# Expert weights in a two-layer diffusion trunk: down rows laid four to a partition, gate/up columns regrouped to match

## The reference, cut to what matters

```python
def expert_choice_ffn(h, w_router, w_gate, w_up, w_down):   # 16 experts, D = D_EXPERT = 1024
    xt = h.reshape(n, D)
    cap = EC_FACTOR * n // N_EXPERTS        # 64 sample tokens or 16 prompt tokens for each expert
    gate, idx = lax.top_k(softmax(xt @ w_router).T, cap)
    xe = jnp.take(xt, idx, axis=0)
    hid = jax.nn.silu(einsum('ecd,edf->ecf', xe, w_gate)) * einsum('ecd,edf->ecf', xe, w_up)
    ye = einsum('ecf,efd->ecd', hid, w_down) * gate[..., None]
    y = zeros.at[idx].add(ye)
```

## Time and profile before

| | |
|---|---|
| median of three runs | 3452.91 us |
| lowest, highest | 3452.17, 3455.37 us |
| the profiled execution, first to last instruction | 3453.8 us |
| TensorE busy | 3344.3 us, 97% |
| VectorE, ScalarE, GpSimd busy | 1257.7, 677.4, 183.0 us |
| mean rate of the DMA engines | 194 GB/s over the span |
| the same in an expert stage | 391 to 393 GB/s |

### The profile page before, as it was taken

One profiled execution on the slowest core, in us unless ns is written; L12 is line 12 of the kernel. 1 busy time (PEld: TensorE's weight loads), 2 busy tenths in 40 slices (PEclk: granted clock), 3 DMA queues, 4 the chain that ended last, 5 costly groups with the idle time before them and its releaser, 6 DMA issues.

```text
span 3453.8 us, 47737 instructions
## 1 busy us (share of the span) xinstructions
PE 3344.3 (97%) x20975; PEld 1901.5 (55%) x20975; DVE 1257.7 (36%) x2317; ACT 677.4 (20%) x1410; POOL 183.0 (5%) x283
## 2 busy tenths in 40 slices
PE   6999999999999899999989999999999998999998
PEld 3557767765654544443355577677656555434433
DVE  3455443436442321212143545433363523111213
ACT  3131111114332300000021311111143322000001
POOL 1000000001100000000100000000011000000000
PEclk9999999999999899999999999999999999999999
DMA  7332332332242799999952324233422418999997
GB/s 224 104 113 66 98 95 65 104 96 90 66 151 80 253 386 390 391 392 385 384 152 78 115 65 122 71 79 90 114 71 92 157 49 310 388 397 390 393 386 300
DMA packets 219086, 669.28 MB, mean 194 GB/s; under 512 B 10574, under 2 KB 24086, under 8 KB 215552
## 3 DMA queue, kind: packets, MB, share of 16 engines
q1 hardware_dynamic: 199200, 613.97, 50.3%
q0 software_dynamic: 13248, 36.65, 3.9%
q10 hardware_dynamic: 6432, 15.62, 1.2%
HBM read 603.04 MB, written 63.15 MB: 193 GB/s over the span
## 4 chain that ended last, share of the span: by engine, by line
PE 91%; DMA 5%; ACT 2%; DVE 1%; issue 1%; SPq 0%; ACTq 0%; DVEq 0%
PE unit L902 13%; PE unit L1426 12%; PE unit L850 11%; PE work L1429 9%; PE work L1426 6%; PE unit L914 4%; PE unit L893 3%; PE unit L933 3%; PE unit L1298 3%; DMA ring<-in_w_e_gate 3%; PE unit L844 3%; PE work L1139 2%; PE work L1105 2%; PE unit L860 1%; PE unit L1251 1%; PE unit L1310 1%
## 5 line engine op out<-in xcount | busy, mean ns | idle before, releaser
L902 PE MATMUL unit<-hT,ring 128*128 128x512 f32 x1024 | 480.2, 597 | 0.0
L1426 PE MATMUL unit<-ring,arena 128*64 128x512 f32 x1568 | 355.2, 598 | 5.4 <-DMA ring<-in_w_e_gate 4.1
L1429 PE MATMUL work<-ring,arena 128*32 128x256 f32 x4608 | 274.8, 382 | 0.4 <-DMA ring<-in_w_e_gate 0.4
L2390 DVE SCALAR_TENSOR_TENSOR arena<-work,arena 32x256 f32<-32x256 f32 x128 | 61.6, 482 | 552.9 <-PE work L1429 551.5
L902 PEld LDWEIGHTS unit<-hT,ring 128*128 128x128 f32 x1024 | 179.0, 192 | 140.1 <-issue 140.1
L1426 PEld LDWEIGHTS unit<-ring,arena 128*64 128x64 f32 x1568 | 109.3, 137 | 226.7 <-issue 214.5
L1429 PEld LDWEIGHTS work<-ring,arena 128*32 128x32 f32 x4608 | 136.8, 109 | 159.8 <-issue 80.4
L850 PE MATMUL unit<-hT,ring 128*128 128x512 f32 x512 | 221.1, 592 | 0.0
L1921 ACT ACTIVATE arena<-work 128x512 f32<-128x512 f32 x32 | 19.1, 597 | 850.3 <-PE work L1443 850.3
L1426 PE MATMUL work<-ring,arena 128*64 128x512 f32 x736 | 166.5, 594 | 2.1 <-ACT arena L1922 2.1
L850 PE MATMUL unit<-arena,ring 128*128 128x512 f32 x384 | 166.8, 592 | 0.0
(11 more groups left out here) (448 smaller groups left out, 4637.2 us busy)
## 6 DMA issues: line engine op xcount, KB each, us to landing
ring<-in_w_e_gate SPq DMA_DIRECT2D x50, 2048.0 KB, 14.8
ring<-in_w_e_up SPq DMA_DIRECT2D x48, 2048.0 KB, 13.8
ring<-in_w_e_down SPq DMA_DIRECT2D x46, 2048.0 KB, 15.3
ring<-in_w_in SPq DMA_DIRECT2D x32, 2048.0 KB, 16.1
ring<-in_w_ada SPq DMA_DIRECT2D x24, 2048.0 KB, 8.7
arena<-in_w_e_down SPq DMA_DIRECT2D x18, 2048.0 KB, 14.1
arena<-in_w_e_up SPq DMA_DIRECT2D x16, 2048.0 KB, 13.5
arena<-in_w_e_gate SPq DMA_DIRECT2D x14, 2048.0 KB, 16.2
```

The costliest lines, as they stand in the source:

```text
L902: last = mm(bank[:, :], w[:, k, m * P:(m + 1) * P], hT[:, k, 0:TS], start=k == 0, stop=k == KD - 1)
L1426: last = mm(big[SLS * c:SLS * c + SLS, :], x, w[:, kk, 512 * c:512 * c + 512], start=k == 0, stop=k == KD - 1)
L1429: last = mm(low[SLOTP * c:SLOTP * c + SLOTP, 0:256], xp, w[:, kk, 256 * c:256 * c + 256], start=k == 0, stop=k == KD - 1)
L2390: STT(y[SLS:SLS + SLOTP, 256 * c:256 * c + 256], W[5][r, 0:256], gpro[r, e:e + 1], gatep[r, :], ALU.mult, ALU.mult)
```

## The change

The load of a down chunk takes the same 512 rows, but partition p now gets the rows 4p to 4p + 3 of the half, which are 16 KB in a row in memory. Block kk of the slot is therefore row 512 half + 4p + kk. The loads of gate and up are as before.

The hidden values have to be turned so that partition p of `hidT` holds these rows. For the samples this is done in `turn_hidden`: tile m takes every fourth column of `hid`. For the prompt tokens it is done earlier: the gate and up matmuls of the narrow part stream their 256 weight columns with a step of four words (16 bytes), two such series after one another, so that the output group c holds the columns 512 (c // 2) + 4a + 2 (c % 2) + m at place 128m + a. The output itself is written in order. The down matmuls stream contiguous columns as before. The numbers of instructions, their widths, the semaphores and their order are the same.

```diff
                 for q, (e, part) in enumerate(MOE):
-                    w = A[dict(g="w_e_gate", u="w_e_up", d="w_e_down")[part[0]]][l, e].rearrange("(k p) n -> p k n", p=P)
+                    w = A[dict(g="w_e_gate", u="w_e_up", d="w_e_down")[part[0]]][l, e]
                     half = int(part[1])
-                    load(l * LAYER_CHUNKS + PRE_CHUNKS + q, w[:, 4 * half:4 * half + 4, :], n=D)
+                    rows = w[512 * half:512 * half + 512, :]
+                    load(l * LAYER_CHUNKS + PRE_CHUNKS + q, rows.rearrange("(p k) n -> p k n", p=P) if part[0] == "d"
+                         else rows.rearrange("(k p) n -> p k n", p=P), n=D)
...
-                                else:
+                                elif kind == "d":
                                     last = mm(low[SLOTP * c:SLOTP * c + SLOTP, 0:256], xp,
                                               w[:, kk, 256 * c:256 * c + 256], start=k == 0, stop=k == KD - 1)
+                                else:
+                                    cols = w[:, kk, 512 * (c // 2):512 * (c // 2) + 512].rearrange("p (a m) -> p m a", m=4)
+                                    out = low[SLOTP * c:SLOTP * c + SLOTP, 0:256].rearrange("p (m a) -> p m a", m=2)
+                                    last = mm(out, xp, cols[:, 2 * (c % 2):2 * (c % 2) + 2, :],
+                                              start=k == 0, stop=k == KD - 1)
...
                     for m in range(4):
-                        tr(W[0][:, tile_t(m)], hid[:, tile_t(m)], ident)
+                        tr(W[0][:, tile_t(m)], hid.rearrange("p (a m) -> p m a", m=4)[:, m, :], ident)
```

## The result

The changed kernel takes 3686.07 us, the median of four runs (3682.90 to 3689.52), against 3453.53 us for the kernel before (3452.17 to 3455.37, four runs). The ratio is 1.0676 with a 95% interval of 1.0661 to 1.0691. The prediction was 3678 us with a range of 3446 to 3712.

A forecast was written before the change was run, and what follows sets the result against it. TensorE was taken as the bound, with the DMA engines just able to follow. 3453.8 + 217 (streamed step) + 11.5 (transposes) - 4.5 (waits) = 3677.8, given as 3678 us (+6.5%), range 3446 to 3712.

The forecast's parts named there:

- What bounds the kernel: Expert stages: TensorE leads, busy 100.00 of 100 us; the DMA engines are just able to follow.
- Part 2: Narrow gate and up blocks: streaming weight columns with a step of four words doubles a column's time, +217 us.
- the row: VectorE's reduction at line 2283, stepping 32 words: 1.74 ns a value, read as a memory limit holding for TensorE too.
- Part 3: Sample transposes: a stepped stationary operand adds up to 90 ns to each of 128 weight loads, +11.5 us.
- Part 1: Down loads in 16 KB runs: 4.5 us of TensorE's waits in the expert stages gone, at most 6.1 us.
- Step free: Rival: stepped gate, up and transpose reads cost 0, only the DMA side is left, 3448 to 3449 us; chance 0.35.
- Partial penalty: Rival: a stepped column in gate and up costs between 0.826 and 1.5 ns, 3465 to 3640 us; chance 0.07.
- shared limit: Rival: the four narrow gate and up streams share one memory limit, +650 us, 4100 us; chance 0.05.
- DMA side worse: Rival: step free, but 16 KB runs load the engines unevenly or gathers wait, 18 us, 3472 us; chance 0.03.

The follow-up runs named there:

- the run on VectorE: Kernel before with VectorE reading the gates at a step of four words when scaling sample results: 3454.91 us, against 3456.32 us before.
- the pairs: Changed kernel with narrow gate and up columns streamed as two adjacent words, then the next pair 16 bytes on: 3465.33 us, ratio 1.0038 to the kernel before.
- the runs with one and two streams: Kernel before with a four-word step in value projections alone (one stream), 3607.06 us, or wide gate and up (two streams), 3926.36 us; before 3451.40.
- two rows to a partition: Kernel before with down rows loaded in 8 KB runs, gate and up streamed contiguously, transposes taking every second column: 3451.59 us, ratio 0.9999.

## Why the prediction was right

**What bounds the kernel.** Right. The expert stage went from 33.71 to 41.3 us an expert with no wait in it; all of the stretch is TensorE's own work.

**Part 2, the streamed step.** Right in place and mechanism, a tenth too small. The term was 217 us; measured are 1.87 us a block x 128 = 239 us. The working value of 1.65 ns a column (a doubling) should have been the row's: with its 1.74 ns the upper bound was +240 us, and 1.74 is what the step's addition to 0.826 ns comes to. Rounding the row down, on the ground that its short loop might have a share, was the error; the run on VectorE, without such a loop, gives 1.81 ns. The reading that decided, that VectorE's 1.74 ns is a limit in ns which TensorE meets too, is confirmed in size on both engines, and as a time by the rounds at the lower clock. That it is one mechanism in the memory is an inference from the nearly equal numbers. The Trainium skill, "SBUF — State Buffer", section "Door 1: The DMA port swizzle", has lines of 16 bytes and a penalty for crossing to a new one; the steps of two, three, four and sixteen words agree with the line. Its sentence that four float32 can be strided for free, read as a step of up to four values, does not agree: a step of two costs 5% of a block (1.95 against 1.86 us), and a step of four doubles it.

**Part 3, the stepped transposes.** Too large: 11.5 us were put down, 3.2 us measured. The weight load grew as costed (+73 ns against +90), but I had taken it for the pace of the four transposes, and it is not: they keep a distance of about 0.15 us where one load lasts 0.21. The rows of before had said so already: 0.123 us a transpose is less than the 0.140 us of a load, so loads overlap one another or the transposes.

**Part 1, the runs of 16 KB.** The waits of 4.5 and 1.6 us are gone in the profile after, and the token gather waits 5.1 us in place of 7.2. The cause was named rightly, a slower TensorE that asks for less: with the streamed step alone and 4 KB pieces the waits for weights are gone as well, while the profile of the 16 KB runs with a fast TensorE has 5.9 us of them. One profile each can say no more, since the term is as small as its own scatter: 0.4 us with the stepped transposes, none with the step of two words or with the pairs. The gather's wait is another matter: it is 7.3 us with the streamed step alone and varies from profile to profile, so its 2.1 us are not shown to be the change's. The 3% that a longer packet gains has no use here. The estimate of 2% from the Trainium skill, "DMA: Bandwidth & Descriptors", section "Why small descriptors are slow (HBM only)", was near that; what it was said to be enough for, the end of the 4.5 us, did not come.

**The sum again, with the measured terms.** 239 + 3.2 - 4.5 - 1.6 - 2.1 = 234 us. The medians differ by 232.5 us. The prediction's total of 3678 us lies within 8 us of the 3686 in part by luck: part 2 was 22 us too small, and part 3 (8 us too large) and the waits not counted (4 us) made up for half of it. The two profiled executions differ by 227.0 us; the one after is the fastest of its four runs and has a mean granted clock of 0.989, while the run of it with 0.985, the clock of the profile before, has a span of 3687.4 us, 233.6 us above.

**The rivals.** Step free: excluded by the two kinds of narrow block in one window. Partial penalty and shared limit: excluded by the block of 3.74 us and by the runs with one and two streams. DMA side worse: 16 KB runs alone cost at most 0.13% by the interval of their ratio.

## What to carry to other kernels

Where TensorE is the bound, look at the order in which a streamed float32 operand is read before laying out anything for the sake of the DMA engines: each column costs its 0.826 ns or the 16-byte units that it newly opens, about 1.75 ns each, whichever is more. So a step of four words or more doubles it, while pairs of adjacent words cost a twentieth. If a permutation has to be absorbed somewhere, the stationary operand of a transpose is the cheaper place: here it was 3 us for 128 transposes. And a shorter transfer is worth at most what the bounding engine waits for it; here that was 6 us, known before.

## What was not expected of the hardware

The price of a stepped value is alike for one, two and four streams of TensorE (1.76, 1.77 and 1.83 ns a column, or 1.74 to 1.75 each without the ends) and nearly so for VectorE (1.81 ns a value). It is a time: it stays nearly the same at half of TensorE's clock (0.90 to 0.96 us a round with two streams), where a contiguous round takes about twice as long (0.85 against 0.44 us). A stationary operand behaves otherwise. With a step of two words the sample transposes' weight load lasts nearly as long as with a step of four, in the kernels with two rows to a partition and with stepped transposes:

```profile
L1449 PEld LDWEIGHTS work<-cst,arena x128: 194/209/219, 1201.9 to 3418.3; 128*128 128x128 f32 x128
```

209 against 213 ns, and 140 contiguous: here two values in one unit do not share it. Why was not tried, and it stays open.
